# Order of the six split products in a k tile of a PE-bound encoder kernel: by token half in place of alternating halves

## The reference

```python
h = _rms(x, p['g_mix_pre'])
proj = h @ p['w_in']                       # split into q1 q2 k1 k2 v ux ug ga gb
...                                        # differential attention, 8 heads, chunk mask
branch_a = o.reshape(B, T, ATTN_V) @ p['w_branch_attn']
...                                        # causal conv, RG-LRU scan
branch_b = (hl * jax.nn.gelu(ug)) @ p['w_branch_lru']
m = jax.nn.sigmoid(ga) * branch_a + jax.nn.sigmoid(gb) * branch_b
x = x + _rms(m @ p['w_out'], p['g_mix_post'])
f = jnp.square(jax.nn.relu(_rms(x, p['g_mlp_pre']) @ p['w_up'])) @ p['w_down']
x = x + _rms(f, p['g_mlp_post'])
```

## Time and profile before

| | |
|---|---|
| median of 3 runs | 2022.09 us (2021.73 to 2027.35) |
| span of the profiled execution, first to last instruction | 2018.6 us |
| median less that span | 3.5 us |
| mean granted TensorE clock | 0.994 of full speed |
| instructions | 38666, of which 15630 matmuls and 15630 weight loads |

### The profile page before, as it was taken

The page is one execution under the profiler, slowest core; times in us unless marked ns, Lnnn a source line. Parts: engine busy times, 40 slices in busy tenths (PEclk is TensorE's granted clock), DMA queues, the critical chain, the costliest instruction groups (busy, mean ns, idle before and its releaser), DMA issues.

```text
span 2018.6 us, 38666 instructions
## 1 busy us (share of the span) xinstructions
PE 1975.9 (98%) x15630; PEld 1929.2 (96%) x15630; DVE 1072.3 (53%) x1986; ACT 955.6 (47%) x1503; POOL 279.1 (14%) x306
## 2 busy tenths in 40 slices
PE   7999999999999999999989999999999999999997
PEld 7999999999998999999989999999999999999997
DVE  6657575765437432333467676767644464224334
ACT  5466666565236431342365757565732554213333
POOL 4312121100101200120041212120001012002100
PEclk9999999999999999999999999999999999999999
DMA  5323232322332323232323232322223323233331
GB/s 136 107 60 105 63 100 69 83 71 78 93 95 70 87 84 93 84 94 84 98 60 98 64 100 72 99 76 75 74 84 94 95 65 92 84 92 86 90 88 67
DMA packets 308455, 172.00 MB, mean 85 GB/s; under 512 B 7592, under 2 KB 303872, under 8 KB 308320
## 3 DMA queue, kind: packets, MB, share of 16 engines
q1 hardware_dynamic: 300768, 155.47, 27.0%
q0 software_dynamic: 7520, 14.59, 2.6%
q10 hardware_dynamic: 32, 0.04, 0.0%
HBM read 158.86 MB, written 11.21 MB: 84 GB/s over the span
## 4 chain that ended last, share of the span: by engine, by line
PE 81%; ACT 9%; DVE 6%; issue 3%; DMA 1%; SPq 0%; ACTq 0%; DVEq 0%
PE PJ L698 65%; PE PJ L710 3%; PE PJ L880 3%; PE PX L908 2%; ACT w_hi L1136 2%; PE PX L926 1%; DVE w_lo L1611 1%; PE PX L946 1%; DVE T L1722 1%; PE PX L962 1%; PE PX L710 1%; DMA w_raw<-in_w_in 1%; DVE uc L1855 1%; ACT L1353 1%; DVE Y L1643 1%
## 5 line engine op out<-in xcount | busy, mean ns | idle before, releaser
L1611 DVE TENSOR_TENSOR w_lo<-w_raw,w_hi 128x1024 fp32r<-128x1024 f32 x284 | 384.2, 1356 | 371.5 <-ACT w_hi L1136 370.4
L698 PE MATMUL PJ<-h_hi,w_hi 128*128 128x272 f32 x2304 | 489.9, 294 | 2.6 <-DVE T L1722 1.9
L698 PE MATMUL PJ<-h_hi,w_lo 128*128 128x272 f32 x2304 | 474.8, 288 | 0.0
L698 PE MATMUL PJ<-h_lo,w_hi 128*128 128x272 f32 x2304 | 473.8, 287 | 0.0
L1136 ACT ACTIVATE w_hi<-w_raw 128x1024 fp32r<-128x1024 f32 x284 | 297.6, 1051 | 233.4 <-DMA w_raw<-in_w_down 116.9
L698 PEld LDWEIGHTS PJ<-h_hi,w_hi 128*128 128x128 f32 x2304 | 359.3, 189 | 12.8 <-issue 9.5
L698 PEld LDWEIGHTS PJ<-h_lo,w_hi 128*128 128x128 f32 x2304 | 360.7, 188 | 0.0
L698 PEld LDWEIGHTS PJ<-h_hi,w_lo 128*128 128x128 f32 x2304 | 359.5, 189 | 0.0
L698 PE MATMUL PJ<-u_hi,w_hi 128*128 128x272 f32 x960 | 198.4, 288 | 0.0
L698 PE MATMUL PJ<-u_hi,w_lo 128*128 128x272 f32 x960 | 197.4, 288 | 0.0
L698 PE MATMUL PJ<-u_lo,w_hi 128*128 128x272 f32 x960 | 197.1, 287 | 0.0
(11 more groups left out here) (351 smaller groups left out, 3595.4 us busy)
## 6 DMA issues: line engine op xcount, KB each, us to landing
w_raw<-in_w_in SPq DMA_DIRECT2D x110, 512.0 KB, 3.8
w_raw<-in_w_down SPq DMA_DIRECT2D x64, 512.0 KB, 3.8
w_raw<-in_w_up SPq DMA_DIRECT2D x62, 512.0 KB, 4.1
w_raw<-in_w_branch_attn SPq DMA_DIRECT2D x16, 512.0 KB, 3.8
w_raw<-in_w_branch_lru SPq DMA_DIRECT2D x16, 512.0 KB, 3.8
w_raw<-in_w_out SPq DMA_DIRECT2D x16, 512.0 KB, 3.8
out_prompt_k<-stage POOLq DMA_DIRECT2D x16, 256.0 KB, 2.8
out_prompt_v<-GA POOLq DMA_DIRECT2D x8, 512.0 KB, 4.5
```

Of the source, the lines that this page charges most:

```text
L698: mm = pe.matmul(PJ[:, buf, half, 0:HT], w[a], src[b][:, k0 + k, HT * half:HT * half + HT], start=first and k == 0 and a + b == 0, stop=en ...
L1611: dve.tensor_tensor(low(n)[:], raw(n), w_hi[:, n.hi, :, :].bitcast(F32), ALU.subtract).then_inc(w_lo_ready, 1)
```

## The change

The six matmuls of a k block are issued in another order. Before, each product is made for the first and then for the second half. After, the first half gets its three products in a row (high-high, high-low, low-high), and then the second half gets its three in the reverse order (low-high, high-low, high-high). The flags that open and close the accumulation in a bank move with the first and the last product of each half. The number of matmuls, their sizes, their operands and the semaphores are the same.

```diff
                     w = (w_hi[:, n.hi, k, :], low(n)[:, k, :])
-                    for a, b in ((0, 0), (0, 1), (1, 0)):
-                        for half in range(2):
-                            mm = pe.matmul(PJ[:, buf, half, 0:HT], w[a], src[b][:, k0 + k, HT * half:HT * half + HT],
-                                           start=first and k == 0 and a + b == 0, stop=end and k == KT - 1 and a == 1)
+                    for half, a, b in ((0, 0, 0), (0, 0, 1), (0, 1, 0), (1, 1, 0), (1, 0, 1), (1, 0, 0)):
+                        opens = (a, b) == ((1, 0) if half else (0, 0))
+                        closes = (a, b) == ((0, 0) if half else (1, 0))
+                        mm = pe.matmul(PJ[:, buf, half, 0:HT], w[a], src[b][:, k0 + k, HT * half:HT * half + HT],
+                                       start=first and k == 0 and opens, stop=end and k == KT - 1 and closes)
                 if ks[-1] == KT - 1:
                     mm.then_inc(tile_done, 1)
```

## The result

The changed kernel takes 2028.74 us (median of 20 runs) against 2022.13 us for the kernel before in the same 20 rounds: +6.6 us, ratio 1.0032, 95% interval 1.0024 to 1.004. It is slower, by just over the 0.3% that was named as the bound. The forecast was 2024 us within 2016 to 2032; the time is inside the range, 4.7 us above the point.

The account below looks back on a forecast made before the run. PE's stream of L698 matmuls was taken to bound the kernel; span 2018.6 plus 2 us for the new order, plus 3.5 us between span and median, gave 2024 us, range 2016 to 2032.

Parts of the forecast that it names:

- What bounds the kernel: Whole kernel: PE busy 98%, L698 alone 65% of the chain, unbroken in the dense MLP and branch projection pieces.
- No instruction, wait or transfer changes: Per k block: the same six matmuls and weight loads, no new wait or DMA, so nothing else moves onto the path.
- The price of the new order: L698's matmul pace, 124.45 ns: bounded between -9.8 and 12.6 us from nearby streams, taken as +2 us.
- the straight line: Middle of L710's paces at 288 and 256 columns: 125.2 ns at 272, 0.7 ns above L698, costing 5.3 us.
- The three differences: Per k block of six: bank changes fall from six to two, weight changes rise from two to three, column-half changes fall to two.
- fewer jumps of the column half save time: L698's moving operand: two half jumps in six instead of six, each saved worth 0.9 ns, -6.6 us; chance 0.10.
- the L880 row: Another line with three products in a row into one bank: 117.3 ns at 256 columns, 0.9 ns less than L710.
- How much lies on the path: 1280 dense k blocks plus 77% of 704 among the attention work, about 1822; one ns each is 1.8 us.
- The slower rival: L698: four steps per k block staying in a bank cost 1.15 ns each, 8.4 us, 2030.5 us; chance 0.21.
- The faster rival: L698: four column-half jumps saved per k block give -3.6 ns, -6.6 us, 2015.5 us; chance 0.10.
- the exposed load: L698: the third weight change shows as one more bare 188 ns load per k block, 343 us, 2365 us; chance 0.03.
- What would show it: MLP piece of 2208 matmuls: 274 to 277 us if right, about 276.5 or more if slower, below 273.5 if faster.

Follow-up runs that it names:

- e8: Kernel before with the loop over halves moved outside the k loop, 24 matmuls of one half in a row; 2048.07 us, ratio 1.0136.
- e5: Changed kernel's order of products and column halves, but the output bank alternates at every step (sums mixed); one run, 2026.9 us against 2021.38 us before.
- e6: Kernel before, column halves alternating, but the output bank stays for three steps (sums mixed); one run, 2021.51 us against 2021.38 us before.
- e9: Changed kernel, but low-activation products read from starts shifted by 4 to 64 columns, by stage (result wrong); one run, 2029.79 us against 2020.37 us before.
- e10: Kernel before, but the second half reads from another start than column 272, by stage (result wrong); one run, 2046.05 us against 2020.37 us before.
- e2: Kernel before, halves and banks still alternating, but the weight part changes three times per k block, not two; 2021.4 us, ratio 0.9996.
- e12: Changed kernel's order with low tiles of h, l, u and high tile of o moved 128 bytes further on; 2034.71 us, ratio 1.006.

## Why the prediction was right or wrong

The time came out inside the range, but the mechanism was missed. The prediction's own last line calls it wrong if the pace moves by more than 0.55 ns; it moved by 0.83.

*What bounds the kernel.* Right: the dense pieces stretched by the price of their matmuls and by nothing else.

*No instruction, wait or transfer changes.* Right: 15630 matmuls and loads, and the same work on the other engines.

*The price of the new order.* This is the step that failed in size: "+2 us: between nothing and the 5.3 us of the straight line, nearer to nothing", which is 1.1 ns per k block. It is 5.0 ns. The straight line between the two widths of L710 gave 125.2 ns for 272 columns, and 125.28 is what came; its excess of 0.73 ns was charged to four steps of six and then cut to less than half, and taken on all six it would have been 4.4 ns. That the line comes so close is in part luck: e8 runs L710's own order at 272 columns, and took 125.69.

*The three differences.* The bank: "a change of bank seems worth nothing", read from `trio`, is right and confirmed by e5 and e6. From it the prediction concluded that the 0.7 ns might come from the widths; this was the wrong turn, since a second thing goes with the bank. That second thing, the column half, was named, but as a possible gain: "fewer jumps of the column half save time". The sign was wrong, on the strength of the L880 row, whose moving operand lies in the weight tiles. e9 and e10 then showed that not the half but its start address counts. The weights: right, no price (e2).

*How much lies on the path.* 77% of the attention's L698 was counted, from its share of the chain; a third of the price reached the end there. A share of the chain says where time was spent in this execution; when that work grows, the chain can move to another engine's work that was nearly as long. That this is what happened here is not shown. With 1280 + 0.34 x 704 = 1520 k blocks at 5.0 ns the sum is 7.6 us. Too low a price and too large a share partly made up for each other, by luck.

*The rivals.* The slower rival gave 2030.5 us for the wrong reason (the bank), with a price, 4.6 ns per k block, that is nearly right. With 5.0 ns the price is beyond the 3.3 from which that rival was to decide, and it had a chance of 0.21. The faster rival and the exposed load did not come about.

*What would show it.* The sign for the slower case, "about 276.5 us or more" in the piece of 2208 matmuls, is what the trace shows (276.62), but the forecast's own 274 to 277 us holds it too, so this sign could not tell the two apart. The other sign of that rival, an excess at the steps inside a half, did not come: over the piece, the four steps inside a half take 126.0, 125.1, 125.0 and 124.3 ns from start to start on average, and the two that change the half 125.6 and 125.7. (Before, the six are uneven too, 122.9 to 125.4.)

## What to carry to other kernels

In a stream that keeps TensorE full, the order of matmuls has a price even when no wait, load or bank conflict is seen: measure it as the pace of a long unbroken piece of the chain, which one profile gives to 0.01 ns, while the time of a launch needed several runs (5 to 20 here) to show 0.3 or 0.4%. When another line of the same kernel runs a similar pattern, its pace is the nearest price: do not cut it for reasons that no row shows, but allow for its error, which was 0.5 ns here (e8 against the straight line), more than half of the effect. And two things that always go together (here the bank and the addresses read) are taken apart by a kernel that changes one of them alone, even if its sums are then mixed, not by argument.

## What was not expected of the hardware

The start addresses of the moving operand changed the pace by up to 2.2% (124.44 to 127.2 ns for 272 columns, e9) with operands that are contiguous in every case. Paces are sharp: 124.44, 125.00, 125.28 and 125.69 ns came back to 0.01 ns in both layers. The same code took 125.3 ns in one layer and 127.2 in the other, and the two paces changed places at a wait (e12). The Trainium skill, TensorE: Matmul & The Clock Gate, section Back-to-back issue gap, gives N / 2.4 + 2.5 ns for an isolated gap, by which an estimate for 272 columns is 115.8 ns, and adds that in a stream the spacing is set by the loads as well. The streams here took more: no pace came below 124.4 ns. The section names no part for the order or the addresses.
